# Recurrent stage of a hybrid decoder trunk: 64x64 products spread over four quadrants, small-rank products a unit ahead, head sums on two banks

## What is computed

```
zm = z + mu * (z_prev - z)
r, k, v, wl, al = jnp.split(zm, RWKV_SPLITS, axis=-1)
w_raw = -jax.nn.softplus(-(w0 + jnp.tanh(wl) @ w_b)) - 0.5
decay = jnp.exp(-jnp.exp(w_raw))
a = jax.nn.sigmoid(a0 + al @ a_b)
kk = k * k_k; kk = kk / max(sqrt(sum(kk * kk, per head)), 1e-12)
k = k * (1 + (a - 1) * k_a)
s = s * decay + (s @ -kk) outer (kk * a) + v outer k      # per token, head
out = s @ r
out = groupnorm(out) * ln_w + ln_b + sum(r * k * r_k, per head) * v
```

## Time and profile before

| | |
|---|---|
| median of 3 runs | 2046.36 us (2042.62 to 2046.47) |
| the profiled execution's own time | 2048.14 us |
| its span | 2046.1 us, mean granted TensorE clock 0.951 |
| TensorE matmuls busy | 1841.1 us |
| VectorE, ScalarE, GpSimd busy | 680.1, 560.5, 368.8 us |
| side work L709 in the whole profile | 576 instructions, 202.3 us |

### The profile page before, as it was taken

How to read it: one execution, slowest core, us unless ns; L and a number is a source line. 1 busy time by engine, 2 the same in 40 slices (tenths; PEclk the granted TensorE clock), 3 DMA queues, 4 the chain that set the end, 5 groups by cost and what they waited for, 6 DMA issues and landing times. The chain is left out here.

```text
span 2046.1 us, 42386 instructions
## 1 busy us (share of the span) xinstructions
PE 1841.1 (90%) x18840; PEld 1228.6 (60%) x18840; DVE 680.1 (33%) x1448; ACT 560.5 (27%) x1148; POOL 368.8 (18%) x438
## 2 busy tenths in 40 slices
PE   7999689999999979689888489888999999899997
PEld 5666465666666645556666478875666666444443
DVE  3101354344443235066666445244120010111122
ACT  4111433334331200166665011122220000122223
POOL 0211331122220000044545211013200010000000
PEclk9999699999999989799999799888999999999999
DMA  4110100000000061350000775436732110400110
GB/s 138 52 31 11 28 3 12 22 13 13 12 13 23 14 149 21 134 125 2 2 2 1 226 231 178 177 101 147 174 85 103 42 41 21 166 21 21 41 41 21
DMA packets 116074, 135.96 MB, mean 66 GB/s; under 512 B 48220, under 2 KB 97061, under 8 KB 111326
## 3 DMA queue, kind: packets, MB, share of 16 engines
q1 hardware_dynamic: 106576, 83.95, 14.9%
q0 software_dynamic: 9216, 49.29, 7.7%
q10 hardware_dynamic: 102, 0.03, 0.0%
HBM read 120.64 MB, written 16.62 MB: 67 GB/s over the span
## 5 line engine op out<-in xcount | busy, mean ns | idle before, releaser
L709 PE MATMUL ps<-xnT,rw_side_w 128*128 128x344 f32 x576 | 202.3, 474 | 0.0
L448 PE MATMUL ps<-xnT,w_z 128*128 128x344 f32 x624 | 183.7, 456 | 2.3 <-DVE xnT L541 1.3
L448 PEld LDWEIGHTS ps<-xnT,w_z 128*128 128x128 f32 x624 | 118.9, 192 | 63.9 <-issue 3.1
L1822 POOL TENSOR_SCALAR probs<-probs,row_sums,gates 128x63 f32<-128x63 f32 (+6 forms) x148 | 95.0, 657 | 291.6 <-DVE row_sums L1782 291.6
L709 PEld LDWEIGHTS ps<-xnT,rw_side_w 128*128 128x128 f32 x576 | 99.5, 190 | 44.6 <-issue 11.1
L2094 PE MATMUL ps<-xnT,zT 128*128 128x344 f32 x384 | 123.9, 473 | 0.0
L2578 PE MATMUL ps<-xnT,ring_k 128*128 128x344 f32 x384 | 116.7, 458 | 2.2 <-PEq L81 2.2
L2582 PE MATMUL ps<-zT,ring_k 128*128 128x344 f32 x384 | 115.0, 452 | 0.0
L2762 PE MATMUL ps<-w_pg,h_T 128*128 128x512 f32 x256 | 111.3, 593 | 1.0 <-ACT h_T L2791 1.0
L2706 PE MATMUL ps<-w_out,mT 128*128 128x512 f32 x256 | 111.6, 593 | 0.5 <-DVE h_sample L2846 0.5
L1166 POOL TENSOR_TENSOR rw_Lb<-rw_Lm,level_mask 128x512 f32<-128x512 f32 x40 | 50.6, 1273 | 271.2 <-DVE rw_Lm L1325 261.2
(11 more groups left out here) (512 smaller groups left out, 2932.5 us busy)
## 6 DMA issues: line engine op xcount, KB each, us to landing
w_z<-in_w_in_dram SPq DMA_DIRECT2D x13, 512.0 KB, 3.8
xnT_kept<-xnT SPq DMA_DIRECT2D x1, 4128.0 KB, 12.7
xnT<-xnT_kept SPq DMA_DIRECT2D x1, 4128.0 KB
...
```

Of the source, the lines that this page charges most:

```text
L448: last = nc.tensor.matmul(k.ps[:, u % 6, 0:CG], w[:, n % w_ring, c, :], k.xnT[:, c, g * CG:(g + 1) * CG], start=(c == 0), stop=(c == KC - 1))
L709: ins = nc.tensor.matmul(k.ps[:, SIDE_BANKS[g % 2], 0:CG], w.side[:, t % 2, c, :], k.xnT[:, c, g % 3 * CG:(g % 3 + 1) * CG], start=(c == 0 ...
L1822: nc.gpsimd.tensor_scalar(every, every, ls[:, at:at + 1], k.gates[:, i, gate:gate + 1], ALU.mult, ALU.mult).then_inc(scaled, 1)
```

## The change

In words: tile 12 is projected first (`Z_TILES`) and its tanh is done inside the projection; the small-rank weights and the first two side weights are loaded there, and the stores of the last rows are no longer waited for at its end. In the recurrent stage, crossed, x_slot and t_slot let a matrix change its half and its slot from level to level, so that each of the products T, XT, X, Gka and the inverse's uses four quadrants. The decayed keys' transposes become 64x64 products. Small-rank products of a unit are made one unit earlier, side by side on banks 4 and 5, in the steps of the unit before; sigmoids, scan and the scale of k move with them, and the exponentials stand at a unit's start. The head sums and their spread use 64x64 weights, four quadrants, banks 4 and 5. The side tables change: 10 matmuls ahead of unit 0, 25 in unit 0, 34 in each later unit, 15 behind. The order of the side tiles changes to gate of attention, gate of recurrence, query. The core of the diff:

```diff
+Z_TILES = (12, 4, 0, 8, 1, 5, 9, 2, 6, 10, 3, 7, 11)
...
+            sp.dma_start(k.lora[0:HD, :], x.rwkv_wB[0]).then_inc(k.in_lora, 16)
+            sp.dma_start(k.lora[HD:P, :], x.rwkv_aB[0]).then_inc(k.in_lora, 16)
+            for i in range(2):
+                load_side(sp, k.side_w, k.in_side, w_rows, i)
...
-            k.stores(sp.dma_start(o.p_shift[0], last_rows[0:1, :]))
-            k.stores(sp.dma_start(o.s_shift[0], last_rows[1:NB + 1, :]))
-            k.stores.wait(sp)
...
+                    if n == Z_FIRST + 2:
+                        act.wait_ge(mixed, 1)
+                        nc.scalar.activation(k.zT[0:HD, ZT - 1, :], k.zT[0:HD, ZT - 1, :], ACT.Tanh).then_inc(lora_in, 1)
...
+SIDE_EARLY = (0, 4, 6, 8, 10)
+SIDE_FIRST = (0, 0, 1, 0, 1, 0, 1, 0, 1, 0, 1, 1, 0, 2, 1, 2, 2, 2, 2, 2, 2, 2, 2)
+SIDE_SLOTS = (3, 1, 1, 0, 1, 1, 1, 1, 1, 1, 1, 1, 2, 2, 1, 2, 2, 2, 2, 2, 2, 2, 2)
+SIDE_LAST = (5, 5, 5)
 
 
 def side_columns(p):
...
-            def lora_w(m):
+            def lora(m):
                 if m:
+                    pe.wait_ge(s.kkd, m)
+                if m >= 2:
...
-                p = m // 2
-                nc.tensor.matmul(k.ps[:, 5, :], w.lora[0:HD, p * P:(p + 1) * P], k.zT[0:HD, 12, tok(m)],
+                p, (b0, b1) = m // 2, lora_banks(m)
+                nc.tensor.matmul(k.ps[:, b0, :], w.lora[0:HD, p * P:(p + 1) * P], k.zT[0:HD, 12, tok(m)],
                                  start=True, stop=True).then_inc(s.lw, 1)
...
+                nc.tensor.matmul(k.ps[:, b1, :], w.lora[HD:P, p * P:(p + 1) * P], k.zT[HD:P, 12, tok(m)],
                                  start=True, stop=True).then_inc(s.la, 1)
...
+            def head_sums(src):
+
+                for i in range(4):
+                    for q in range(2):
+                        for r in range(2):
+                            at = r * (HT // 2) + i * HD
+                            last = nc.tensor.matmul(k.ps[half(r), 4 + q, 2 * i:2 * i + 2], src[half(q), at:at + HD],
+                                                    k.ones[half(q), 0:2], start=True, stop=True)
+                return last
+
+            def norm_rows(src):
+
+                for i in range(4):
+                    for q in range(2):
+                        for r in range(2):
+                            n = 4 * q + i
+                            last = nc.tensor.matmul(k.ps[half(q), 4 + r, i * HD:(i + 1) * HD],
+                                                    src[half(r), n:n + 1].broadcast_to((HD, HD)), k.ident[half(r), half(r)],
+                                                    start=True, stop=True)
+                return last
...
+            def crossed(n):
+
+                for i in range(4):
+                    for a in range(2):
+                        for e in range(2):
+                            if n % 2:
+                                q, cp = i % 2, i // 2 * 2 + a
+                                yield q, e, cp, e ^ q ^ a, a, q * 2 + cp // 2
+                            else:
+                                yield a, e, i, e, a, i
...
+            def x_slot(n, q, cp):
+
+                return q * 4 + cp if n == 0 else (q ^ cp & 1) * 4 + q * 2 + cp // 2
+
+            def t_slot(n, q, cp):
+
+                return (cp & 1) * 4 + q * 2 + cp // 2 if n % 2 else q * 4 + cp
...
+            pe.wait_ge(k.in_lora, 32)
+            lora(0)
+            sample_lora()
             k_sumsq(0)
-            sample_lora()
+            side(-1, 0)
+            sample_sumsq()
+            side(-1, 1)
             k_norm(0)
+            side(-1, 2)
+            lora(1)
             bonus(0)
-            sample_sumsq()
+            side(-1, 3)
...
+                side(m, 0)
...
                     if q:
-                        last = nc.tensor.matmul(k.ps[half(1 - e), 3, cp * HD:(cp + 1) * HD], w.RA[hq, z, 1, c, :],
+                        last = nc.tensor.matmul(k.ps[half(1 - e), 3, 256 + cp * HD:256 + (cp + 1) * HD], w.RA[hq, z, 1, c, :],
                                                 w.BK[hq, z, 0, c, :], start=True, stop=True)
...
+                if m == 0:
+                    pe.wait_ge(s.bond, 1)
+                for hq, he, q, e, cp, c in chunks():
+                    if q:
+                        for n, h in enumerate((he, half(1 - e))):
+                            last = nc.tensor.matmul(k.ps[h, 1, cp * P + n * HD:cp * P + (n + 1) * HD], w.BK[hq, z, 0, c, :],
+                                                    w.RA[hq, z, n, c, :], start=True, stop=True)
+                    else:
+                        last = nc.tensor.matmul(k.ps[he, 0, cp * P:(cp + 1) * P], w.BK[hq, z, 0, c, :], w.RA[hq, z, :, c, :],
+                                                start=True, stop=True)
                 last.then_inc(s.u, 1)
+                side(m, 1)
...
-                for cp in range(4):
-                    last = nc.tensor.transpose(k.ps[:, 2, cp * P:(cp + 1) * P], w.RA[:, z, 1, 2 * cp:2 * cp + 2, :], k.ident[:])
+                for hq, he, q, e, cp, c in chunks():
+                    last = nc.tensor.matmul(k.ps[half(e ^ q), 2 + q, cp * HD:(cp + 1) * HD], w.RA[hq, z, 1, c, :],
+                                            k.ident[hq, hq], start=True, stop=True)
...
-                side(m, 0)
...
+                    for q, e, cp, h, f, i in crossed(n):
+                        last = nc.tensor.matmul(k.ps[half(h), f, i * HD:(i + 1) * HD], w.Lb[half(e ^ q), n % 2, q * 4 + cp, :],
+                                                w.XT[half(e ^ q), t_slot(max(n - 1, 0), q, cp), :], start=True, stop=True)
...
+                    if n == 1:
...
+                    elif n == 2:
...
-                        for he, u, q, cp in units():
-                            last = nc.tensor.matmul(k.ps[he, 2, u * HD:(u + 1) * HD], w.Gka[he, q, cp, :], w.V[he, q, cp, :],
-                                                    start=True, stop=True)
+                        for hq, he, q, e, cp, c in chunks():
+                            last = nc.tensor.matmul(k.ps[half(e ^ q), 2 + q, cp * HD:(cp + 1) * HD], w.Gka[he, q, cp, :],
+                                                    w.V[he, q, cp, :], start=True, stop=True)
...
                     elif n == 3:
...
-                    for q, e, cp, u in crossed():
-                        last = nc.tensor.matmul(k.ps[half(e), q, 256 + cp * HD:256 + (cp + 1) * HD], w.X[half(e ^ q), u, :],
-                                                w.T1[half(e ^ q), u, :], start=True, stop=True)
-                    if n < 4:
-                        for q, e, cp, u in crossed():
-                            last = nc.tensor.matmul(k.ps[half(e ^ q), 3, u * HD:(u + 1) * HD], w.T1[half(e ^ q), u, :],
-                                                    w.X[half(e ^ q), u, :], start=True, stop=True)
...
-                    if n == 0:
-                        if m:
-                            mean(m - 1)
-                    elif n == 1:
+                        pe.wait_ge(s.y_out, m + 1)
...
+                    elif n == 4:
...
+                    pe.wait_ge(s.x_out, lv + 1)
+                    if n == 1 and m:
+                        mean(m - 1)
+                    elif n == 2 and m:
+                        variance(m - 1)
+                    elif n == 4 and after:
+                        k_sumsq(m + 1)
+                    side(m, 2 * n + 2)
+                    if n == 3 and m:
                         rstd(m - 1)
-                    side(m, 2 * n + 2)
+                    pe.wait_ge(s.t_out, lv + 1)
+                    for q, e, cp, h, f, i in crossed(n):
+                        last = nc.tensor.matmul(k.ps[half(e ^ q), f, 256 + i * HD:256 + (i + 1) * HD],
+                                                w.X[half(h), x_slot(n, q, cp), :], w.T1[half(h), t_slot(n, q, cp), :],
+                                                start=True, stop=True)
+                    last.then_inc(s.xtp, 1)
+                    side(m, 2 * n + 3)
+                    if n == 4 and after:
+                        k_norm(m + 1)
+                    if n < 4:
+                        if n == 0:
+                            pe.wait_ge(s.gka, m + 1)
+                        elif m:
+                            pe.wait_ge((s.cent, s.vard, s.xnd)[n - 1], m)
+                        for hq, he, q, e, cp, c in chunks():
+                            f = cp & 1 if n % 2 else q
+                            d = q ^ cp & 1
+                            h, j = half(e ^ q ^ f), q * 2 + cp // 2
+                            last = nc.tensor.matmul(k.ps[half(e ^ q ^ f ^ d), 4 + d, j * HD:(j + 1) * HD],
+                                                    w.T1[h, t_slot(n, q, cp), :], w.X[h, x_slot(n, q, cp), :],
+                                                    start=True, stop=True)
+                        last.then_inc(s.x, 1)
...
-                for he, u, q, cp in units():
```

(7 more changed lines are left out.)

471 lines of the change are left out of this document (223 added, 248 removed).

## The result

The changed kernel takes **1970.5 us** (median of 4 runs, 1967.8 to 1973.6) against 2046.4 of the kernel before in the same set: ratio 0.964, 95% interval 0.961 to 0.968. The profiled execution took 1972.8, its span is 1970.8.

A forecast was written before the change was run, and what follows sets the result against it. TensorE, 90% busy with matmuls, was taken as the bound. Terms of 50.6 + 5.2 - 2 + 6.5 + 11.3 = 71.6 us off the profiled 2048.14, less 1.8 for the median, gave 1975; 8-in-10 range 1957 to 2004.

The forecast's parts named there:

- The likeliest case: Whole kernel: four quadrants for two and side work in idle places bring 1975 us, range 1962 to 1990; chance 0.68.
- unit 0: First recurrent unit: 25 side matmuls added, 4.8 us of other work removed; 44.0 to 46 us, 2 lost.
- the start: Ahead of unit 0: weights already there, TensorE starts at about 215.3, unit 0 at 231.5 instead of 237.97; 6.5 us gained.
- six units: Units 1 to 6: 53.0 us each instead of 61.4, 368.6 to 318 us in all; 50.6 us gained.
- The small-rank pair: Two products side by side in each unit, 1.05 us each before; gain between none and 1.05, taken as 0.5.
- The waits: TensorE's waits in a unit: T 0.7 and X 0.8 in level 0, key sum in level 4 1.0; 1.5 us less than before.
- 1 (levels bound by the chain): Levels, seven units: copies on ScalarE or masks on VectorE hold TensorE, 35 us come back, 2010 us; chance 0.13.
- 2: X, Gka, inverse's product: row halves writing one bank go one after the other, 27 us come back, 2002 us; chance 0.04.
- 3: Head sums: two-column sums priced by the instruction, 3.7 us each, 51 us come back, 2026 us; chance 0.04.
- 4 (the clock falls in the levels): Levels of every unit: TensorE's clock at 0.50, eight units cost 112 us more, 2087 us, slower than before; chance 0.02.
- 6 (units of 50.5, 1958 us): Units: the three forecast waits don't appear and the average of 61.4 was mostly waits; 1958 us; chance 0.09.
- 5 (less at the ends): Stage's ends: clock low ahead of unit 0, side copies late; 1985 us, inside the forecast's own range, no separate chance.

The follow-up runs named there:

- lora_split: The changed kernel with a unit's two small-rank products in two separate steps instead of side by side; 1975.6 us, 0.9668 of the kernel before.
- loads_late: The changed kernel with small-rank and first side weight loads back in the recurrent stage, behind the wait for stores; 1976.0 us, 0.9665 of the kernel before.

## Why the prediction was right, and where it was not

**The likeliest case came in:** 1975 predicted, 1970.5 measured, with the mechanism as described, four quadrants for two. That it came so close is in part luck: of the terms, unit 0 is 6.9 us worse than forecast, and the start (2.3), six units (5.3) and unit 7 (1.9) are together 9.5 better. Its terms in a unit, as measured: X 2.0 (predicted 2.0), Gka 0.5 (0.5), the inverse's product 1.96 to 1.05 (1.10), spreads 1.0 (1.0), head sums 0.7 (0.8: 0.57 each and not 0.52).

**The small-rank pair was mis-sized:** "each is two instructions, issued in order: from no gain to 1.05. I take 0.5." It is 1.05, the upper bound (lora_split). By the rows, issued in order does not mean started in order.

**Six units** gained 55.9, not 50.6. The forecast had added 1.2 us to unit 4's sum since the old units were longer than it on average. Unit 4 came to 52.3 (51.8 before that surcharge) and the mean to 52.1. The surcharge, 7.2 us in six units, was wrong and is more than the whole difference of 5.3. In unit 4 the terms of the list add to 6.3 and not 5.7. Side work gave 0.5 and not 1.0, and XT, T and the transposed keys, which I had left as they were, take 0.85 more between starts.

**The waits** were forecast as 0.7, 0.8 and 1.0. T's in level 0 came to 0.84 (0.7), X's to 0.33 (0.8), and the key sum's chain in level 4 did not appear (1.0). In their place stands one that I did not have: 0.89 us in level 0 for the second addition, which since the move of L1220 waits for GpSimd. I had asked who waits for L1220, not what it runs beside. The sum, 2.1 for 2.5, is right by compensation.

**Unit 0 is the step that failed:** "Now 28 - 4.8 + 14.3 + 3 is 40.5, with waits of 3.5 and a stretch at the lower clock 46." It took 52.9: TensorE's work takes 45.0 us between starts and its waits 7.9, at a granted clock of 1.00 throughout, so the 2 us for the lower clock weren't needed.

- Waits, 4.4 more than forecast: 2.9 are those for T behind the sampled operations (worth 2.3 to 2.6 of the unit), 1.4 the one for XT in level 0 that depends on which engine comes first. A wait of 1.33 for unit 0's first mask was not tried; scan and scale of the next unit (1.2 and 0.5 us of VectorE) now stand ahead of it and would fit.
- Side work, 2.2 more: 19.5 for 17.3. Three side matmuls, 1.9 us by the timeline, belong to unit 1 but stand ahead of its first product and so within this distance, 28 and not 25.
- The other groups, 2.3 more: 25.5 for 28 - 4.8 = 23.2. The 28 was too small; unit 4's groups of before without side work and norm take 29.1 between starts, and the product of the sampled bonus 0.9.

I had guessed the waits, and left VectorE's new order out.

**Unit 7** gained 7.1 for 5.2. It holds the matmuls of its first slot no longer, for the same reason as above: 31 side matmuls and not 34, which is most of the difference.

**The start** was 2.3 us earlier than forecast, 0.1 in another execution. TensorE's first product stands at 213.0 and not at 215.3, and at 215.2 in that other one; from there to unit 0 it takes 16.1 and 16.3, for the forecast's 15 to 16. So the difference comes from the stage before. What the early loads are worth in it is shown (loads_late). **The end** fits: 14.7 for 14.5.

**The rivals.** 1 (levels bound by the chain): in units 1 to 6 only level 0 waits. 2 and 3 are refuted by the 0.51 of X, which writes each of its two banks from both row halves, and by the 0.57 of a sum. The first also differs from the rule of the Trainium skill (TensorEngine Tiling (Array Packing), Restrictions and Gotchas) on row tiles and one bank, the second from its 60 cycles for each matmul (Performance Considerations), by which a sum was estimated at 0.8; in both the measurement decides. 4 (the clock falls in the levels) does exist, at one or two hundredths of the size: in level 0 of unit 2, behind waits of 0.82 and 0.89 us, TensorE had the lower clock for some 3 us, and the unit took 53.0 instead of 52.0. Other units have the same waits and the clock stays at 1.00.

```profile
341.00:344.00 3.00, 3.00 (x71) 2.07 (x74) 1.56 (x4) 0.60 (x1) 2.92 (x3) 0.53 0.00 0
```

6 (units of 50.5, 1958 us) was no outcome of the change, but is where its units arrive without the two blocked additions: 50.6. 5 (less at the ends) did not come.
